# Operands of float32r matmuls at other places modulo 512 bytes, in a two-block transformer on one core

## What is computed

```python
# first block: layer 0 an mLSTM mixer, layer 1 latent attention (MLA); each followed by a gated FFN
hl, hc = modulate(x, ...), modulate(ctx, ...)
yl, yc = mlstm(hl, hc) ; yl = mla(hl, hc)          # layer 1 needs no context output
x  = layer_norm(ALPHA * x + gate * yl)
x  = layer_norm(ALPHA * x + gate * ((silu(dwconv(h @ w_gate)) * (h @ w_up)) @ w_out))   # width 2816
# second block: 10-part projection, convolution / differential attention / gating mixers, then an MLP
z  = split(modulate(rms_norm(x)) @ w_in, 10)
x  = x + gate * (token_mixers(z, k1, k2, v) @ w_out)
x  = x + gate * (square(relu(h @ w1)) @ w2)                                             # width 4096
return rms_norm(x)                                  # the latents alone
```

## The kernel before

| tile | before | after |
|---|---|---|
| `raw`, `w_hi`, `w_lo`, `ada_ring` | 128 | 0 |
| `h0_*`, `m_*`, `hs`, `h_*`, `hid_*`, `ckv_*`, `cq_*`, `xv`, `qk` | 192 | 0 |
| `conv`, `probs`, `vtok` | 160 | 480 |
| `h_*`, `hid_*` where the latents alone are packed | - | 64 |

## Time and profile before

### The profile page before, as it was taken

How to read it: one execution, slowest core, us unless ns; L and a number is a source line. 1 busy time by engine, 2 the same in 40 slices (tenths; PEclk the granted TensorE clock), 3 DMA queues, 4 the chain that set the end, 5 groups by cost and what they waited for, 6 DMA issues and landing times.

```text
span 2482.3 us, 30985 instructions
## 1 busy us (share of the span) xinstructions
PE 2379.6 (96%) x12204; PEld 1937.1 (78%) x12204; DVE 1652.8 (67%) x2686; ACT 987.2 (40%) x1534; POOL 30.7 (1%) x64
## 2 busy tenths in 40 slices
PE   7999999999999999999998998999999999988997
PEld 3878877866677888887758997766788888767997
DVE  6776567345368886778558778487666565677664
ACT  2422232236443321223554444465432232456543
POOL 0000000010000000000000000000000000000000
PEclk9999999999999999999999999999999999999999
DMA  8355534452153445343404553211245345323553
GB/s 320 110 189 203 187 136 159 180 215 91 68 191 116 144 155 192 131 157 104 149 20 139 190 183 128 68 51 51 93 154 211 136 164 191 100 74 113 180 188 126
DMA packets 95803, 357.16 MB, mean 144 GB/s; under 512 B 10969, under 2 KB 11353, under 8 KB 93353
## 3 DMA queue, kind: packets, MB, share of 16 engines
q1 hardware_dynamic: 93082, 339.37, 39.0%
q0 software_dynamic: 2576, 15.82, 1.8%
HBM read 349.90 MB, written 5.24 MB: 143 GB/s over the span
## 4 chain that ended last, share of the span: by engine, by line
PE 72%; issue 16%; DVE 8%; ACT 3%; DMA 1%; POOL 0%; SPq 0%; POOLq 0%; DVEq 0%; ACTq 0%
PE PS L545 57%; PE PS L573 3%; PE PS L707 3%; PE PS L902 2%; DVE w_lo L1633 1%; PE PS L1065 1%; ACT w_hi L1090 1%; PE PS L825 1%; PE PS L843 1%; PE PS L818 1%; DVE conv L2281 1%; DMA ada_ring<-in_ada 1%; DVE ada_ring L1649 0%; PE PS L660 0%; ACT wgt L1221 0%
## 5 line engine op out<-in xcount | busy, mean ns | idle before, releaser
L1633 DVE TENSOR_TENSOR w_lo<-raw,w_hi 128x1024 fp32r<-128x1024 f32 (+1 forms) x456 | 543.3, 1209 | 341.1 <-ACT w_hi L1090 339.7
L1090 ACT ACTIVATE w_hi<-raw 128x1024 fp32r<-128x1024 f32 (+1 forms) x456 | 461.1, 1041 | 475.9 <-PE PS L545 466.4
L545 PE MATMUL PS<-h_hi,w_hi 128*128 128x512 f32 (+1 forms) x1432 | 485.5, 339 | 17.4 <-DVE h_lo L1742 9.0
L545 PE MATMUL PS<-h_lo,w_hi 128*128 128x512 f32 (+1 forms) x1432 | 484.1, 338 | 0.0
L545 PE MATMUL PS<-h_hi,w_lo 128*128 128x512 f32 (+1 forms) x1432 | 483.7, 338 | 0.0
L545 PEld LDWEIGHTS PS<-h_hi,w_hi 128*128 128x128 f32 x1432 | 270.6, 189 | 50.8 <-issue 12.8
L545 PEld LDWEIGHTS PS<-h_lo,w_hi 128*128 128x128 f32 x1432 | 270.5, 189 | 30.5 <-issue 0.2
L545 PEld LDWEIGHTS PS<-h_hi,w_lo 128*128 128x128 f32 x1432 | 270.7, 189 | 29.9
L545 PE MATMUL PS<-hid_hi,w_hi 128*128 128x512 f32 (+1 forms) x864 | 290.1, 336 | 2.8 <-DVE w_lo L1633 2.8
L545 PE MATMUL PS<-hid_lo,w_hi 128*128 128x512 f32 (+1 forms) x864 | 290.1, 336 | 0.0
L545 PE MATMUL PS<-hid_hi,w_lo 128*128 128x512 f32 (+1 forms) x864 | 289.1, 335 | 0.0
(11 more groups left out here) (366 smaller groups left out, 3608.2 us busy)
## 6 DMA issues: line engine op xcount, KB each, us to landing
raw<-in_weights SPq DMA_DIRECT2D x434, 512.0 KB, 4.5
ada_ring<-in_ada SPq DMA_DIRECT2D x176, 512.0 KB, 3.7
raw<-in_weights SPq DMA_DIRECT2D x22, 384.0 KB, 4.0
qk<-in_ada SPq DMA_DIRECT2D x4, 1024.0 KB, 10.7
xv<-in_ada SPq DMA_DIRECT2D x4, 1024.0 KB, 12.8
m_hi<-h_spill POOLq DMA_DIRECT2D x4, 1024.0 KB, 7.8
wgt<-in_x SPq DMA_DIRECT2D x2, 1024.0 KB, 22.4
h_spill<-h_hi POOLq DMA_DIRECT2D x1, 2048.0 KB, 8.9
```

Source lines behind the costliest of these rows:

```text
L545: mm = pe.matmul(out, a, b, start=(k == 0 and i == 0), stop=(k == ph.k_tiles - 1 and i == 2))
L1090: act.activation(w_hi[:, s, 0:w], raw[:, s, 0:w], ACT.Copy).then_inc(sem("w_hi"), 1)
L1633: dve.tensor_tensor(w_lo[:, s, 0:w], raw[:, s, 0:w], w_hi[:, s, 0:w].bitcast(F32), ALU.subtract)\
```

## The change

Three things are changed, all of them addresses. (1) The small tiles are allocated first and `raw` is put at a multiple of 512, and so are `m_hi`, `m_lo`, `h_hi` and `hid_hi`; what follows them in the row lands there too, since their sizes are multiples of 512. (2) The gap ahead of `h_hi` goes. (3) `packed()` gives a phase of the latents alone its operand as 256 columns at `64 + 1024 * k` bytes from the tile's start, where before it was the latents' half of row k, at `1024 + 2048 * k`. That holds for aout, f1, wo1 and g1: for PE's reads and for the writes by ACT and DVE. dq, zg1 and z1 read the latents' half as before (`hl`), as other products read the same tile in full; uqn and uqr read `cq_*`.

```diff
+OFF_LINE = 16
...
-        def sb(name, shape, dt=F32, stack=ctx):
-            return stack.enter_context(nc.sbuf_tensor(name, shape, dt))
-
-        def behind_line(name, gap, stack):
-
-            stack.enter_context(nc.sbuf_tensor(name, [P, gap // 4], F32, align_bytes=LINE))
+        def sb(name, shape, dt=F32, stack=ctx, line=32):
+            return stack.enter_context(nc.sbuf_tensor(name, shape, dt, align_bytes=line))
...
-        raw = sb("raw", [P, RING, UNIT])
-        w_hi = sb("w_hi", [P, RING, UNIT], F32R)
-        w_lo = sb("w_lo", [P, RING, UNIT], F32R)
...
         eps = sb("eps", [P, 1])
+        raw = sb("raw", [P, RING, UNIT], line=LINE)
+        w_hi = sb("w_hi", [P, RING, UNIT], F32R)
+        w_lo = sb("w_lo", [P, RING, UNIT], F32R)
...
-            m_hi = sb("m_hi", [P, 16, T], F32R, st)
+            m_hi = sb("m_hi", [P, 16, T], F32R, st, LINE)
...
-                m_lo = sb("m_lo", [P, 16, T], F32R, inner)
+                m_lo = sb("m_lo", [P, 16, T], F32R, inner, LINE)
...
-            behind_line("gap_h", 192, st)
-            h_hi = sb("h_hi", [P, 8, T], F32R, st)
+            h_hi = sb("h_hi", [P, 8, T], F32R, st, LINE)
...
-                hid_hi = sb("hid_hi", [P, 16, T], F32R, inner)
+                hid_hi = sb("hid_hi", [P, 16, T], F32R, inner, LINE)
...
+        def packed(tensor, i):
+
+            flat = tensor[:].rearrange("p t n -> p (t n)")
+            return flat[:, OFF_LINE + i * CTX:OFF_LINE + (i + 1) * CTX]
+
+        def columns_at(tensor, i, full, cols=slice(0, T)):
+            return tensor[:, i, cols] if full else packed(tensor, i)
...
-            hx = lambda full: (lambda k: h_hi[:, k, rng(full)], lambda k: h_lo[:, k, rng(full)])
-            hid = lambda full: (lambda k: hid_hi[:, k, rng(full)], lambda k: hid_lo[:, k, rng(full)])
+            hx = lambda full: (lambda k: columns_at(h_hi, k, full), lambda k: columns_at(h_lo, k, full))
+            hl = (lambda k: h_hi[:, k, LAT], lambda k: h_lo[:, k, LAT])
+            hid = lambda full: (lambda k: columns_at(hid_hi, k, full), lambda k: columns_at(hid_lo, k, full))
...
-            residual_product("aout", *hl, False, True, ready=[("att_e", 16), ("o_lo", 7)], each=("o_lo", 0))
+            residual_product("aout", *hx(False), False, True, ready=[("att_e", 16), ("o_lo", 7)], each=("o_lo", 0))
...
-                    front(("zg1",), *hx(False), ("h_lo", 8 * 6))
-                    linear("zg1", *hx(False))
+                    front(("zg1",), *hl, ("h_lo", 8 * 6))
+                    linear("zg1", *hl)
...
-                    act.activation(h_hi[:, Y_ORDER[p], r], TMP[:, p % 4, r], ACT.Copy).then_inc(sem("y_hi"), 1)
+                    act.activation(columns_at(h_hi, Y_ORDER[p], full), TMP[:, p % 4, r], ACT.Copy).then_inc(sem("y_hi"), 1)
...
```

More of the change, by code:

```diff
@@ L281, in sem @@
             return sems[name]
-        raw = sb("raw", [P, RING, UNIT])
-        w_hi = sb("w_hi", [P, RING, UNIT], F32R)
-        w_lo = sb("w_lo", [P, RING, UNIT], F32R)
-        ada_ring = sb("ada_ring", [P, ADA_RING, D])
-        ada_junk = sb("ada_junk", [P, D])
-        crow = sb("crow", [P, 2, D])
         mod_dot = sb("mod_dot", [P, 2, 48, 2])
@@ L298, in two_stacks @@
         eps = sb("eps", [P, 1])
+        raw = sb("raw", [P, RING, UNIT], line=LINE)
+        w_hi = sb("w_hi", [P, RING, UNIT], F32R)
+        w_lo = sb("w_lo", [P, RING, UNIT], F32R)
+        ada_ring = sb("ada_ring", [P, ADA_RING, D])
+        ada_junk = sb("ada_junk", [P, D])
+        crow = sb("crow", [P, 2, D])
         with ExitStack() as st:
@@ L795, in _ @@
             feed_forward("f0", True, 1)
-            hl = (lambda k: h_hi[:, k, LAT], lambda k: h_lo[:, k, LAT])
             front(("dkv", "dkr"), *hx(True), ("h_lo", 16))
@@ L887, in _ @@
                 per_head = len(slots) // 4
-                z_hi, z_lo = hx(full)
+                z_hi, z_lo = hx(True) if full else hl
+                y_part = hx(full)
                 def z_tile(step):
@@ L1048, in _ @@
                 item[0] += len(slots)
-                y_hi, y_lo = (lambda p: z_hi(Y_ORDER[p])), (lambda p: z_lo(Y_ORDER[p]))
+                y_hi, y_lo = (lambda p: y_part[0](Y_ORDER[p])), (lambda p: y_part[1](Y_ORDER[p]))
                 def y_products(g, m, c):
@@ L1305, in h_tiles @@
                     for i, (c, v) in enumerate(halves(full)):
-                        ins = act.activation(h_hi[:, t, c], TMP[:, t % 4, c], ACT.Identity,
+                        ins = act.activation(columns_at(h_hi, t, full, c), TMP[:, t % 4, c], ACT.Identity,
                                              bias=mod[:, par, 8 * chunk + t, v:v + 1])
@@ L1333, in conv_ffn @@
                         act.wait_ge(sem("free_dve"), ph.free0 + 2 * f + 2)
-                        act.activation(hid_hi[:, f, r], TMP[:, 4 + f % 2, r], ACT.Copy).then_inc(sem("hid_hi"), 1)
+                        act.activation(columns_at(hid_hi, f, full), TMP[:, 4 + f % 2, r], ACT.Copy).then_inc(sem("hid_hi"), 1)
                         if half == 0 and f < 8:
@@ L1349, in hi @@
                         act.wait_ge(sem("prod"), base - 44 + i + 1)
-                        act.activation(hid_hi[:, i, r], TMP[:, 4 + i % 2, r], ACT.Copy).then_inc(sem("hid_hi"), 1)
+                        act.activation(columns_at(hid_hi, i, full), TMP[:, 4 + i % 2, r], ACT.Copy).then_inc(sem("hid_hi"), 1)
                     def relu(i, t):
@@ L1415, in o_hi @@
                 act.wait_ge(sem("att_o"), h + 1)
-                act.activation(h_hi[:, h, LAT], PS[:, out_bank(h), 0:CTX], ACT.Copy).then_inc(sem("o_hi"), 1)
+                act.activation(columns_at(h_hi, h, False), PS[:, out_bank(h), 0:CTX], ACT.Copy).then_inc(sem("o_hi"), 1)
             only_split("uqr")
@@ L2015, in lo @@
                     for c, v in halves(full):
-                        ins = dve.scalar_tensor_tensor(out=h_lo[:, t, c], in0=TMP[:, t % 4, c], scalar=scalar(par, chunk, t, v),
-                                                       in1=h_hi[:, t, c].bitcast(F32), op0=ALU.add, op1=ALU.subtract)
+                        ins = dve.scalar_tensor_tensor(out=columns_at(h_lo, t, full, c), in0=TMP[:, t % 4, c], scalar=scalar(par, chunk, t, v),
+                                                       in1=columns_at(h_hi, t, full, c).bitcast(F32), op0=ALU.add, op1=ALU.subtract)
                     ins.then_inc(sem("h_lo"), 1)
@@ L2068, in lo @@
                         dve.wait_ge(sem("hid_hi"), base + f + 1)
-                        dve.tensor_tensor(hid_lo[:, f, r], TMP[:, 4 + f % 2, r], hid_hi[:, f, r].bitcast(F32), ALU.subtract)\
+                        dve.tensor_tensor(columns_at(hid_lo, f, full), TMP[:, 4 + f % 2, r], columns_at(hid_hi, f, full).bitcast(F32), ALU.subtract)\
                             .then_inc(sem("hid_lo"), 1)
@@ L2169, in o_lo @@
                 dve.wait_ge(sem("o_hi"), h + 1)
-                dve.tensor_tensor(h_lo[:, h, LAT], PS[:, out_bank(h), 0:CTX], h_hi[:, h, LAT].bitcast(F32), ALU.subtract)\
+                dve.tensor_tensor(columns_at(h_lo, h, False), PS[:, out_bank(h), 0:CTX], columns_at(h_hi, h, False).bitcast(F32), ALU.subtract)\
                     .then_inc(sem("o_lo"), 1)
@@ L2230, in lo @@
                         dve.wait_ge(sem("hid_hi"), base + i + 1)
-                        dve.tensor_tensor(hid_lo[:, i, r], TMP[:, 4 + i % 2, r], hid_hi[:, i, r].bitcast(F32), ALU.subtract)\
+                        dve.tensor_tensor(columns_at(hid_lo, i, full), TMP[:, 4 + i % 2, r], columns_at(hid_hi, i, full).bitcast(F32), ALU.subtract)\
                             .then_inc(sem("hid_lo"), 1)
@@ L2350, in y_lo @@
                     j = Y_ORDER[p]
-                    dve.tensor_tensor(h_lo[:, j, r], TMP[:, p % 4, r], h_hi[:, j, r].bitcast(F32), ALU.subtract)\
+                    dve.tensor_tensor(columns_at(h_lo, j, full), TMP[:, p % 4, r], columns_at(h_hi, j, full).bitcast(F32), ALU.subtract)\
                         .then_inc(sem("y_lo"), 1)
```

## The result

The changed kernel takes 2470.81 us (median of 4, 2470.26 to 2474.42) against 2490.66 of the kernel before (4 executions, 2488.27 to 2494.13): a ratio of 0.9922, 95% interval 0.9907 to 0.9936, so 0.6 to 0.9% faster. The forecast was 2455 with a range of 2415 to 2510; the narrower range of the forecast's own mechanism, 2440 to 2470, is missed by 0.8. The profiled execution took 2470.89 us, 13.2 less than that of before.

What follows compares the result with a forecast made beforehand. PE was taken as the bound: float32r matmul count times start-to-start distance. Savings of 12.3 + 8.0 + 9.0 = 29.3 us off the profiled 2484.0 gave 2454.7, forecast as 2455 us, range 2415 to 2510.

Steps and rivals of the forecast that it cites:

- What bounds the kernel: Whole kernel: in the large stretches, time is the number of float32r matmuls times their start-to-start distance; PE busy 96%.
- Part 1: 512-column activations moved from 192 to 0, weights from 128 to 0: 5544 matmuls reach 226.7 ns, saving 12.3 us.
- Part 2: Products with weights as moving operand (v, og, ukv), from 128 to 0: 1200 matmuls save 6.7 ns each, 8.0 us.
- Part 3: Packed latents in aout, f1, wo1, g1, from 192 to 64: 2019 matmuls go from 117.8 to 113.3, saving 9.0 us.
- Part 4: Unpacked 256-column products (dq, uqn, uqr, zg1, z1), 564 matmuls from 192 to 0: costed at 0, 2.5 us either way.
- Part 5: DVE, ACT and DMAs write at other places: costed at 0, covered by DVE's slack and weight slots waiting for PE.
- the prediction's own sign: Wrong in kind if f0's distance rises, or if a stretch with fixed addresses still shows both paces.
- Only parts 2 and 3 act: Rival, chance 0.14: 192 already as good as 0 for activations; token-major saves 5.3, latents 9.0, giving 2470 us.
- Places do not matter: Rival, chance 0.17: pace set by the moment PE resumes after a wait; time wanders 2484 to 2494, about 2488 us.
- The line is the worse place: Rival, chance 0.20: moving read and weight load meet at 0, 512-column activations slow by 24.6 us; 2500 to 2515 us.
- Full relief: Rival, chance 0.07: a stream beginning on a line loses nothing, only 2.5 ns remain; saves 117 us, giving 2367.
- roles exchanged: The prediction's reading of f0 (228.9 ns) against v (233.3), where weights move instead of activations; raised under a rival.

Runs made afterwards that it cites:

- the benches: Kernels of float32r matmuls alone, moving and stationary operands at varied byte places, behind different pauses; at distance 0 the later table has 226.7 to 227.9 ns (512 columns).

## Why the prediction was right, and where it was wrong

**What bounds the kernel**: held. PE is busy throughout the long stretches, and nanoseconds per matmul came out as microseconds at the end: the sum below comes within 1 us of the difference of the profiled executions.

**Part 1** (12.3 us): the size held to the tenth, the reason did not. f0 and g0 save 2.2 ns per matmul, at 226.7. That value was taken as twice the best 256-column pace, and that it came is luck: at distance 0, where 512 columns take 226.7, 256 columns take 120.0, their worst multiple of 64, and at 192, where they reach 113.3, 512 columns take 233.3. The prediction also rested on the moving operand's own place modulo 512; what acts is its distance from the stationary slice.

**Part 2** (8.0 us): held. v saves 6.6 ns per matmul.

**Part 3** (9.0 us) is the step that failed, "If 64 holds the better pace". The packed operand lay 64 bytes beyond the weights before and lies 64 beyond them now, so nothing was changed for the matmul, and it drew from the same two paces: f1 kept 117.8, and g1, at 113.3 in the profile of before, drew 117.8. 1485 matmuls were at 113.3 before, and 133, all in wo1, in the changed kernel. That is 1352 x 4.44 = 6.0 us lost in place of 9.0 gained, near the bound of that part (6.6).

**Part 4** (0): 516 matmuls went from 117.8 to 120.0 and 48 of z1 from 113.3, 1.5 us lost, inside its bounds of 2.5.

**Part 5** (0): held; DVE's `h_lo` of 256 columns takes 478 ns with the packed target where it took 477:

```profile
L2021 DVE SCALAR_TENSOR_TENSOR h_lo<-xv,mod,h_hi 128x256 fp32r<-128x256 f32 x96 | 42.7, 478 | 3.0 <-ACT h_hi L1311 3.0
```

The sum as it came: -12.3 - 8.0 + 6.0 + 1.5 = -12.8 us, against -13.2 between the two profiled executions. The forecast of 29.3 was over twice that. The medians are 19.9 us apart, as the profiled execution of before lies 4.2 to 10.1 us under the others; that these had g1 at the slower pace fits the sizes, but they have no trace. So the choice to start from the fastest execution known and not to add its 4.5 us back carried the forecast further off, and that the measured time still lies inside 2415 to 2510 owes as much to the width of that range as to the mechanism. By the prediction's own sign it is wrong in kind: with fixed addresses wo1 still shows both paces.

**The rivals.** "Only parts 2 and 3 act" named the time that came, 2470, and by none of its reasons: part 1, which it had at nothing, gave the most, part 2 gave 6.6 ns and not 4.4, and part 3 lost. "Places do not matter" is refuted for 512 columns, and fits the latents in this change. "The line is the worse place" had the right quantity in view, the 64 bytes between the two operands, and the wrong sign for 512 columns; for 256 columns the sign is right, distance 0 is the worst multiple of 64. "Full relief" never came: no distance gave less than 226.6 or 113.3 ns. The rule of the Trainium skill ("TensorE: Matmul & The Clock Gate", section "Wait — 56ns, not 53.3ns?", N / 2.4 GHz + 2.5 ns) does not hold for float32r with a new stationary slice for each matmul: 215.8 against 226.6 to 237.8. And where the Trainium skill ("SBUF — State Buffer", section "Who interferes with whom") has PE wait for no one, PE's pace here depends on how its own two operands lie to each other, with one small ACT operation per case and no DVE work in the benches.

**What should have been seen.** The rows had two distances for 512 columns, 64 and -64, and I set them aside as "roles exchanged". Had the distance been tabulated beside the places, part 3 would have read "64 before, 64 after" and been costed at zero.

## What to carry to other kernels

Where float32r matmuls alternate with weight loads back to back, tabulate the moving operand's byte minus the stationary slice's, modulo 256, for every product: 0 for 512 columns, 112 or 192 for 256 columns, met exactly (4 bytes beside them it was 115.5 to 122.1 ns). It costs no instruction, only fillers in the allocation. Between multiples of 16 bytes it was worth up to 4% of a matmul for 512 columns and 6% for 256, and 1.2% of this kernel. And before a difference of under 1% is put down to an edit, look whether the same code shows two paces in one trace.

## What was not expected of the hardware

The start-to-start distance of float32r matmuls at full clock is 13 to 24 ns over one column per cycle for 512 columns (226.6 to 237.8 against 213.3) and 6.6 to 23 ns for 256 (113.3 to 129.6 against 106.7). At multiples of 64 bytes the distance between PE's two SBUF operands modulo 256 sets it, with no DVE work beside it. At 1.2 GHz the excess is gone (213 ns for 256 columns, seen at distance 64 alone). At distances 64 and 192 two paces exist for 256 columns, 113.3 and 117.8; every change from one to the other that was looked at stands at a pause, and between pauses a pace was kept for over a thousand matmuls. 512 columns have a second pace too, which the distance does not explain: in the kernel before, three of z0's 16 tiles ran at 233.3 at distance 64 and the others at 228.9, where none of the benches' cases at 64 was over 229.3; at 112 the bench has 226.6 and 231.5 by turns. At distance 0 none of the large 512-column products settled at another pace than 226.7. What makes all this was not found: that the weight load's read and the moving operand's collide is a guess that no run tested, as none took the weight loads away.
